# SSD scan of a bidirectional Mamba-2 layer: both state sweeps first and with priority, then the diagonal passes with the closing of each chunk inside them

## The reference

```python
def ssd_scan(x, dt, A, Bm, Cm, h0):          # chunks of CHUNK = 128 tokens
    ...
    decay = jnp.exp(jnp.where(mask, seg, -jnp.inf))          # seg = cs[l] - cs[s]
    CB = jnp.einsum("bclgn,bcsgn->bclsg", Cc, Bc)
    y_diag = jnp.einsum("bclsg,bclsgr,bcsgr,bcsgrp->bclgrp", CB, decay, dtc, xc)
    states = jnp.einsum("bclgn,bclgr,bclgrp->bcgrpn", Bc, decay_to_end * dtc, xc)
    def step(h, inp):                         # over the chunks, in order
        s, d = inp
        return h * d[..., None, None] + s, h
    h_final, h_starts = lax.scan(step, h0, (states, chunk_decay))
    y_off = jnp.einsum("bclgn,bcgrpn,bclgr->bclgrp", Cc, h_starts, jnp.exp(cs))
    return y_diag + y_off, h_final

y = y_f + flip(y_b) + d_skip[:, None] * xs    # forward and backward scan
y = y * silu(z)
return rmsnorm(y, norm_w) @ w_out, hf, hb
```

## Time and profile before

| | us |
|---|---|
| runs shown | 3765.62 and 3832.91, median 3799.26 |
| the profiled execution | 3770.94 |
| its span, slowest core (core 5) | 3769.4 |
| spans of all cores | 3744.1 to 3769.4 |
| PE busy | 2735.3 (73%) |
| DVE busy | 1370.6 (36%) |
| ACT busy | 1176.1 (31%) |
| mean granted TensorE clock, core 5 | 0.887 |

### The profile page before, as it was taken

One profiled execution on the slowest core, in us unless ns is written; L12 is line 12 of the kernel. 1 busy time (PEld: TensorE's weight loads), 2 busy tenths in 40 slices (PEclk: granted clock), 3 DMA queues, 4 the chain that ended last, 5 costly groups with the idle time before them and its releaser, 6 DMA issues.

```text
span 3769.4 us, 45170 instructions; the slowest of 8 cores (3744.1 to 3769.4 us)
## 1 busy us (share of the span) xinstructions
PE 2735.3 (73%) x16592; PEld 1372.2 (36%) x16592; DVE 1370.6 (36%) x1889; ACT 1176.1 (31%) x1510; POOL 282.2 (7%) x302
## 2 busy tenths in 40 slices
PE   1586666666879886799868666656686989687895
PEld 0243333332435442345434333333243544243452
DVE  0215554646342004322031565555634210414202
ACT  1325444455132013321023545445423200323201
POOL 1110000000011100011100000000000111000010
PEclk9688888978989998899979898888898999798998
DMA  9451202011448860369733111102034886222452
GB/s 150 57 70 26 37 21 31 34 26 29 49 60 105 83 105 3 40 79 105 80 35 48 27 31 26 34 23 31 32 40 54 103 89 62 62 28 32 53 56 67
DMA packets 412214, 200.17 MB, mean 53 GB/s; under 512 B 189408, under 2 KB 395360, under 8 KB 412000
## 3 DMA queue, kind: packets, MB, share of 16 engines
q0 software_dynamic: 391840, 151.28, 36.0%
q1 hardware_dynamic: 20160, 46.01, 3.4%
HBM read 322.30 MB, written 26.21 MB: 92 GB/s over the span
## 4 chain that ended last, share of the span: by engine, by line
PE 54%; DVE 17%; ACT 14%; issue 7%; DMA 7%; DVEq 0%; ACTq 0%; POOL 0%; POOLq 0%; SPq 0%
PE pa L419 50%; ACT arena L432 11%; DVE arena L439 7%; DVE arena L442 6%; DMA arena<-ada_w 3%; PE pm L419 3%; ACT arena L447 2%; DVE arena L504 2%; PE pm L423 1%; DMA arena<-mlp_w 1%; DMA arena<-ssd_w_in 1%; DVE pa L439 1%; DMA arena<-init_st 1%; ACT L432 1%; DVEq L285 0%
## 5 line engine op out<-in xcount | busy, mean ns | idle before, releaser
L419 PE MATMUL pa<-arena 128*128 128x512 bf16 (+3 forms) x13200 | 2626.8, 347 | 588.9 <-DVE arena L439 236.4
L419 PEld LDWEIGHTS pa<-arena 128*128 128x128 bf16 x13200 | 1174.2, 101 | 1726.1 <-issue 975.8
L439 DVE TENSOR_TENSOR arena<-arena 128x512 bf16<-128x512 bf16 (+2 forms) x784 | 518.2, 685 | 743.9 <-ACT arena L432 596.1
L432 ACT ACTIVATE arena<-pa 128x512 bf16<-128x512 f32 (+2 forms) x491 | 393.2, 820 | 802.6 <-PE pa L419 775.2
L432 ACT ACTIVATE arena<-arena 128x1280 bf16<-128x1280 f32 (+6 forms) x295 | 301.6, 1043 | 1050.7 <-DVE arena L442 1017.8
L419 PE MATMUL pm<-arena 128*128 128x2 bf16 (+3 forms) x2632 | 383.0, 202 | 327.3 <-ACT arena L432 133.1
L442 DVE SCALAR_TENSOR_TENSOR arena<-pa,arena 128x1279 f32<-128x1279 f32 (+2 forms) x160 | 205.3, 1283 | 821.5 <-PE pa L419 529.7
L419 PEld LDWEIGHTS pm<-arena 128*128 128x128 bf16 x2632 | 216.7, 103 | 483.1 <-issue 422.0
L447 ACT ACTIVATE arena<-pa 128x512 bf16<-128x512 f32 (+2 forms) x368 | 217.2, 612 | 282.2 <-PE pa L419 254.5
L442 DVE SCALAR_TENSOR_TENSOR arena<-arena 128x1024 f32<-128x1024 f32 (+4 forms) x306 | 205.7, 683 | 93.3 <-ACT arena L432 65.2
L96 POOL DMA_DIRECT2D arena<-mlp_w x128 | 129.0, 1008 | 1046.0 <-PE pa L419 448.2
(11 more groups left out here) (13 smaller groups left out, 109.9 us busy)
## 6 DMA issues: line engine op xcount, KB each, us to landing
arena<-mlp_w POOLq DMA_DIRECT2D x128, 512.0 KB, 7.1
arena<-ada_w POOLq DMA_DIRECT2D x96, 512.0 KB, 6.4
st_out<-arena SPq DMA_DIRECT2D x80, 256.0 KB, 2.1
arena<-ssd_w_in POOLq DMA_DIRECT2D x32, 512.0 KB, 6.0
arena<-ssd_w_out POOLq DMA_DIRECT2D x16, 512.0 KB, 6.7
arena<-dftA SPq DMA_DIRECT2D x16, 512.0 KB, 5.2
arena<-xT SPq DMA_DIRECT2D x8, 640.0 KB, 11.5
yT<-arena SPq DMA_DIRECT2D x8, 640.0 KB, 3.0
```

Source lines behind the costliest of these rows:

```text
L419: P.op("pe", lambda e: e.matmul(out, lhsT, rhs, start=start, stop=stop, skip_group_check=True), reads, writes, cost=0.06 + fsz(out) / 2400.0)
L432: P.op("act", lambda e: e.activation(out=out, in_=in_, func=func, **kw), reads, writes, cost=0.22 + fsz(out) / 1200.0)
L439: P.op(eng, lambda e: e.tensor_tensor(out=out, in0=in0, in1=in1, op=op), reads, writes, cost=vcost(eng, out))
```

## The change

The scan of a group is written in another order and its chunks are closed in another place. First all ten pairs of sweep steps are recorded, with priority 1; the scheduler gets that priority in place of 0. In them the first direction to reach a chunk writes its scaled output straight to `hb_bf[:, c]` (key `yoS`), the second writes `yo` and adds it. Then ten diagonal passes are recorded with priority 0, in the order 4, 5, 3, 6, 2, 7, 1, 8, 0, 9. Each ends with the identity products of `xD` and of `hb_bf[:, c]`, the copy to `y_tm`, the four transposes and the product with `ygT`.

```diff
+        self.prio = 0
...
-            bl = [0.0] * n
+            bl = [float(o["prio"]) for o in ops]
...
-                    def diag_pass(c):
+                    def diag_pass(c, par):
...
-                        mm(Yb, ident, xD, False, True, ["cb", "xD"], [YK])
-                        cp("act", hb_bf[:, c, :], Yb, [YK], [("stash", c)])
+                        mm(Yb, ident, xD, False, False, ["cb", "xD"], [YK])
+                        mm(Yb, ident, hb_bf[:, c, :], False, True, ["cb", ("yoS", c)], [YK])
+                        y_tm = y_tm2[par]
+                        ytk = ("y_tm", par)
+                        cp("act", y_tm, Yb, [YK], [ytk])
+                        for t_ in range(4):
+                            tr(PM[1][:, t_ * 128:(t_ + 1) * 128], y_tm[:, t_ * 128:(t_ + 1) * 128], [ytk], [PMK[1]], t_ == 0)
+                        ygv = ygT[:, g * 4:(g + 1) * 4, ck]
+                        gkeys = [("ygT", g * 4 + t_) for t_ in range(4)]
+                        tt("dve", ygv, PM[1][:, 0:512].rearrange("p (t l) -> p t l", t=4), ygv, ALU.mult, [PMK[1]] + gkeys, gkeys)
...
-                        if finalize:
...
-                            mm(Yf, ident, hb_bf[:, c, :], True, False, ["cb", ("stash", c)], [YfK])
-                            mm(Yf, ident, yo[d], False, True, ["cb", ("yo", d)], [YfK])
-                            cp("act", y_tm, Yf, [YfK], [ytk])
...
+                        if not second:
+                            tt("dve", hb_bf[:, c, :]..., ob..., e_offk..., ALU.mult, [ok_, "e_offk"], [("yoS", c)])
                         else:
-                            tt("dve", hb_bf[:, c, :], hb_bf[:, c, :], yo[d], ALU.add, [("stash", c), ("yo", d)], [("stash", c)])
+                            tt("dve", yo[d]..., ob..., e_offk..., ALU.mult, [ok_, "e_offk"], [("yo", d)])
+                            tt("dve", hb_bf[:, c, :], hb_bf[:, c, :], yo[d], ALU.add, [("yoS", c), ("yo", d)], [("yoS", c)])
...
-                    for stp in range(NCH // 2):
-                        diag_pass(stp)
-                        diag_pass(NCH - 1 - stp)
-                        sweep_step(1, NCH - 1 - stp, finalize=False)
-                        sweep_step(0, stp, finalize=False)
-                    for stp in range(NCH // 2, NCH):
-                        sweep_step(1, NCH - 1 - stp, finalize=True)
-                        sweep_step(0, stp, finalize=True)
+                    P.prio = 1
+                    for stp in range(NCH):
+                        cb_ = NCH - 1 - stp
+                        cf_ = stp
+                        sweep_step(1, cb_, second=(cb_ < NCH // 2))
+                        sweep_step(0, cf_, second=(cf_ >= NCH // 2))
+                    P.prio = 0
+                    npass = 0
+                    for k in range(NCH // 2):
+                        for c in (NCH // 2 - 1 - k, NCH // 2 + k):
+                            diag_pass(c, npass % 2)
+                            npass += 1
```

More of the change, by code:

```diff
@@ L85, in _add @@
         self.ops.append(dict(eng=eng, fn=fn, deps=sorted(deps), odeps=sorted(odeps), chan=chan, cost=cost,
-                             phase=self.phase, fill=(self.fill if (eng == "pe" and chan is None) else None), gap=0.0))
+                             phase=self.phase, fill=(self.fill if (eng == "pe" and chan is None) else None), gap=0.0,
+                             prio=self.prio))
         return idx
@@ L839, in state_out @@
                         P.dma("sp", st_d[u, j, d][:, g * 512:(g + 1) * 512], H[d], reads=[("H", d)], chan=("sto", d))
-                    def diag_pass(c):
+                    def diag_pass(c, par):
                         ck = slice(c * 128, (c + 1) * 128)
-                        par = c % 2
                         Yb, YK = Yd[par], YKd[par]
@@ L872, in diag_pass, with sweep_step @@
                            d_bc[:, hs].unsqueeze(2).to_broadcast([128, 8, 64]), ALU.mult, ["x_tm", "rows"], ["xD"])
-                        mm(Yb, ident, xD, False, True, ["cb", "xD"], [YK])
-                        cp("act", hb_bf[:, c, :], Yb, [YK], [("stash", c)])
-                    def sweep_step(d, c, finalize):
+                        mm(Yb, ident, xD, False, False, ["cb", "xD"], [YK])
[8 more added lines that the diff above has]
+                        tt("dve", ygv, PM[1][:, 0:512].rearrange("p (t l) -> p t l", t=4), ygv, ALU.mult, [PMK[1]] + gkeys, gkeys)
+                    def sweep_step(d, c, second):
                         ck = slice(c * 128, (c + 1) * 128)
@@ L896, in sweep_step @@
                         mm(ob, CgT[:, ck], hbf, True, True, ["CgT", hbk], [ok_])
-                        tt("dve", yo[d].rearrange("p (h q) -> p h q", h=8), ob.rearrange("p (h q) -> p h q", h=8),
-                           e_offk[:, d, c, hs].unsqueeze(2).to_broadcast([128, 8, 64]), ALU.mult, [ok_, "e_offk"], [("yo", d)])
-                        if finalize:
[L900 to L904, removed]
-                            mm(Yf, ident, hb_bf[:, c, :], True, False, ["cb", ("stash", c)], [YfK])
-                            mm(Yf, ident, yo[d], False, True, ["cb", ("yo", d)], [YfK])
-                            cp("act", y_tm, Yf, [YfK], [ytk])
[L908 to L912, removed]
-                        else:
-                            tt("dve", hb_bf[:, c, :], hb_bf[:, c, :], yo[d], ALU.add, [("stash", c), ("yo", d)], [("stash", c)])
+                        if not second:
+                            tt("dve", hb_bf[:, c, :].rearrange("p (h q) -> p h q", h=8), ob.rearrange("p (h q) -> p h q", h=8),
+                               e_offk[:, d, c, hs].unsqueeze(2).to_broadcast([128, 8, 64]), ALU.mult, [ok_, "e_offk"], [("yoS", c)])
+                        else:
+                            tt("dve", yo[d].rearrange("p (h q) -> p h q", h=8), ob.rearrange("p (h q) -> p h q", h=8),
+                               e_offk[:, d, c, hs].unsqueeze(2).to_broadcast([128, 8, 64]), ALU.mult, [ok_, "e_offk"], [("yo", d)])
+                            tt("dve", hb_bf[:, c, :], hb_bf[:, c, :], yo[d], ALU.add, [("yoS", c), ("yo", d)], [("yoS", c)])
                         state_update(d, c)
```

## The result

The changed kernel takes 3859.39 us (median of 9 runs), the kernel before 3803.84 (median of 8). Runs in which the cores of one die ran at a lower clock than the others are in these two medians, but left out of every ratio and of every time given for an experiment; without them the kernel before took 3765.57 to 3774.78 us. The ratio is 1.0239, with a 95% interval of 1.0225 to 1.0253. The profiled execution took 3860.42 us, 89.5 more than that of before; its span is 3858.6.

A forecast was written before the change was run, and what follows sets the result against it. It took the scan as bound by chains from engine to engine, with no engine full. It summed 8 x (13.9 - 1.3) - 15 = 86 us onto 3770.9, giving 3857, rounded 3860 us; range 3795 to 3965.

The forecast's parts named there:

- The sweeps: Sweep steps of a scan, alone from the end of C's Silu: 48.4 us, between 45 and 56.
- The start: Opening of the sweeps: second pair's state copies after about 4.5 us, the first pair's two yo adding 1.2.
- the start state: Direction 1's store and load in the sweeps: a wait of 4 us, between 2 and 7.
- Pairs of the second half: Five pairs of second comers in the sweeps, two adds more each: 4.6 us a pair.
- The passes: Nine passes in a row behind the sweeps: 8.4 us each, 75.6, then 1.1 to the last product into `ygT`.
- The closing: End of each pass: second identity product 0.22, copy and waits 0.95, transposes 0.2, together 1.37 us.
- The straight line: Pass time against TensorE's clock, from chunk 9's passes: 8.0 us at 0.5, 6.5 at 1.0, without closing.
- the prediction's own test: Called the forecast wrong if a pass takes under 8.0 or over 9.0 us, or the sweeps over 56.
- the two gains at the edges: One table load fewer on each scan's path, 1.3 us; next group's projection products earlier, 2.5 us in six scans.
- Rival 1: TensorE's clock stays low in the passes, mean 0.6: a pass takes 9.3 us, kernel 3937 us; chance 0.20.
- Rival 2: Fused pass is short, 7.8 us at full clock, and the start state's wait filled: 3785 us; chance 0.12.
- Rival 4: Change doesn't do what it says, priority might not bring sweeps ahead; or both orders cost alike: 3771 us; chance 0.04.

The follow-up runs named there:

- experiment 5: Changed kernel with the copy to `y_tm`, transposes and `ygT` product recorded behind the next pass's first two Exps: 3784.69 us, ratio 1.0037.
- experiment 1: Changed kernel with the sweeps' priority set to 0 in place of 1: 3867.19 us, ratio 1.0259.
- experiment 3: Changed kernel with `xD` reading `x_tm` under its own key, passes at priority 1 and sweeps at 0: 3767 to 3784 us, ratio 1.0008.
- 8: Changed kernel with the late closing and direction 1's start state loaded early into another buffer, sweeps still alone: 3756.38 us, ratio 0.9966.
- 9: Changed kernel with own key for `xD`, passes at priority 1 and sweeps at 0, late closing and early start state: 3684.08 us, ratio 0.9778.
- 11: Kernel before with one pass and one pair of sweep steps alternating, early start state, late transposes and own key for `xD`: 3713.07 us, ratio 0.9859.

## Why the prediction came out as it did

The time was right (3860 predicted, 3859.39 measured), and so was the place: a scan is longer by 14.5 us on the slowest core and by 13.4 on the mean of all, against 13.9. The terms inside were not, and that the total came out to 1 us is luck.

**The sweeps: 48.4 predicted, 55.0 in group 1.** Direction 1's products with C come 5.0, 7.6, 18.3, 21.4, 25.6, 29.6, 33.8, 38.4, 43.6 and 50.1 us after C's Silu. The start was 1.8 us too short: the second pair's state copies begin at 5.5 for my 4.5, and the first pair's two yo are done at 7.5 for 5.7. The step from 7.6 to 18.3 holds the start state; it is 10.7, 6.7 more than a step of 4.0, where I took 4 from bounds of 2 and 7. On most other cores that step is about 8.5, 4.5 more, so the 4 was near the mark and core 3 is the exception; by the mean of the cores the sweeps take 53.1. Pairs of the second half take 4.2, 4.6, 5.2, 6.5 and 4.9, where I took 4.6 each; the 6.5 has the memset for a new sequence in it. That chain runs at a product of 0.58 in place of 0.38 us; that the clock's fall makes the pairs longer is likely, but no run separates it.

**The passes: 8.4 predicted, 7.65 measured.** The closing was right: 0.84 us of wait a pass for the 0.95 I took, and closing late gave back 1.1. The pass without it was read too long: 7.07 us from chunk 9's at clocks of 0.70 and 0.87 with xw products in VectorE's queue, while the lone one runs at 1.00 and takes 7.3 with its closing. The straight line of the prediction had 6.5 for a pass at full clock, and with the closing behind the next Exps it is 6.38 (experiment 5). By the prediction's own test (under 8.0) this term was wrong. Nine passes with their end took 71.8 for 76.7. The last pass hides a third term: with its 1.1 us of ending it is 10.6 us, and TensorE makes products of the next group's projection between its own. Scans with no group behind them in the layer, which have none of these, are 2.8 us shorter than the others (124.7 and 127.5; before, 112.4 and 113.8). So about 1.4 of the 2.5 us counted as a gain there come back as a longer scan, and the stretches between scans gave 18 us where the two gains at the edges were put at 25.

So +6.6 for the sweeps and -4.9 for the passes nearly cancelled: 55.0 + 1.9 + 71.8 = 128.7 against 127.4. The total says less for the working than it seems to.

**The rivals.** Rival 1, a low clock in the passes, fell: 0.93 over eight of them, with 0.74 in the first, 0.79 in the seventh and 1.00 in the other six. The Trainium skill (TensorE: Matmul & The Clock Gate, section HAM oscillation) tells of a kernel in which the waits for DMA between bursts of matmuls bring the low clock back each time; those waits are much longer than the 0.84 us that six passes here have at 1.00, so no run here tests it. Rival 2 had the right pass (7.8, under 8.2) and the wrong sum, since it also took the start state's wait as filled, and the sweeps came out longer and not shorter. Rival 4 said that priority might do nothing. For this change that is so (experiment 1), and I had taken the row of 34 products for proof of it: the order shows what stands where, not why. The sweeps are ahead by the chain of `x_tm`.

**What makes it slower.** The prediction's reason, that the steps filled holes that a pass has anyway, is shown from both ends: letting two and a half passes back among the sweeps removes the whole loss (experiment 3), and with the two other waits gone, mixing is still worth 70 us (8 and 9). It is not the only account, though: the late closing alone takes off 75 us with the sweeps still apart (5). The change lost by separating the two kinds of work and by a closing on the path of each pass, and repairing either is enough to be back near the time before. This is the direction in which the Trainium skill points (Perfetto Trace Analysis, section Optimization Strategy), and the runs now give it a size; one to one, though, was no better than a third (9 against 11), but those two kernels also close their chunks in different places, so mixing alone isn't what they compare.

## What to carry to other kernels

Two kinds of work that are bound by chains can cost less side by side than one behind the other, even where VectorE is 80% busy in one of them, as here; before separating them, ask what fills the holes of each. Where each engine has a fixed order, a step that closes a unit is worth trying behind the first work of the next unit: here that was 1.1 us a pass, 75 us in all. And where a recorder keeps readers of one key in order, look for the key before the priority: a row in the order doesn't tell which of the two put it there.

## What the runs showed of the hardware

- In 50.2 us of sweeps, in which TensorE made 61 products and waited between them, its granted clock was 0.55, near the lower level, and most products took 0.58 us in place of 0.38. Eight passes with 372 products in 61.2 us ran at 0.93, though the engine stood 0.84 us in each for the copy.
- A store and a load through one buffer took 9.6 us from the copy to the first product, and 7.8 before: 3.5 us from the first store's issue to the load's (2.2 before), of which SP spent 1.65 issuing two stores (0.94 before), and 4.0 from there to ScalarE's copy (3.5 before). These are single scans of core 3 and core 5.
